# Small parameter rows ahead of the bulk loads on one queue, in a one-core inference step

## The reference

```
mod = silu(cond) @ ada_w + ada_b            # 6 vectors of 1024 each, for context and for latents
h   = rmsnorm(x) * norm1_g * (1 + sc1) + sh1
z   = h @ w_in                              # 1280 columns: 512 state space, 256 pooling, 512 convolution
y   = concat(ssm(z), pool(z), conv(z)) @ w_out
x   = x + g1 * y
h2  = rmsnorm(x) * norm2_g * (1 + sc2) + sh2
x   = x + g2 * ((silu(h2 @ w1) * (h2 @ w3)) @ w2)
out = rmsnorm(x) * final_g
```

## Time and profile before

| quantity | value |
|---|---|
| median of 3 runs | 1314.56 us (1313.19 to 1315.68) |
| the profiled execution, timed | 1311.89 us |
| its span, first to last instruction | 1310.0 us |
| PE busy | 1219.5 us (93%) |
| DVE, ACT, POOL busy | 857.4, 510.2, 521.7 us |
| mean granted TensorE clock | 0.975 of full speed |
| DMA | 268.52 MB, mean 205 GB/s |

### The profile page before, as it was taken

One profiled execution on the slowest core, in us unless ns is written; L12 is line 12 of the kernel. 1 busy time (PEld: TensorE's weight loads), 2 busy tenths in 40 slices (PEclk: granted clock), 3 DMA queues, 4 the chain that ended last, 5 costly groups with the idle time before them and its releaser, 6 DMA issues.

```text
span 1310.0 us, 21433 instructions
## 1 busy us (share of the span) xinstructions
PE 1219.5 (93%) x7574; PEld 1072.3 (82%) x7574; DVE 857.4 (65%) x1336; ACT 510.2 (39%) x911; POOL 521.7 (40%) x362
## 2 busy tenths in 40 slices
PE   3888899996699999899999999999999999999996
PEld 2478898786446888899999999999889999999995
DVE  2647959989944337667767666766855555555558
ACT  1464451126245547533333433433432333333223
POOL 0179425554343003455444445444533333333330
PEclk9889999997799999999999999999999999999998
DMA  8833345389872333766666576566677778777781
GB/s 273 313 110 120 114 140 177 102 109 229 270 290 97 104 121 102 252 226 229 219 208 211 189 256 224 213 219 220 237 232 250 240 260 277 255 249 264 242 279 73
DMA packets 189569, 268.52 MB, mean 205 GB/s; under 512 B 14030, under 2 KB 108536, under 8 KB 186824
## 3 DMA queue, kind: packets, MB, share of 16 engines
q1 hardware_dynamic: 187952, 263.00, 61.8%
q0 software_dynamic: 1280, 4.72, 0.9%
q10 hardware_dynamic: 280, 0.09, 0.0%
HBM read 186.49 MB, written 81.26 MB: 204 GB/s over the span
## 4 chain that ended last, share of the span: by engine, by line
PE 79%; DVE 8%; ACT 3%; DMA 3%; issue 3%; POOL 2%; SPq 1%; ACTq 0%; DVEq 0%; POOLq 0%
PE banks L891 22%; PE banks L893 22%; PE banks L892 22%; PE banks L1163 3%; PE banks L927 1%; PE banks L1042 1%; PE banks L976 1%; DMA dn<-in_ssm_d 1%; POOL sst L820 1%; PE banks L1059 1%; PE banks L1065 1%; PE banks L962 1%; ACT nts L1700 1%; DVE dsel L1959 1%; PE banks L935 1%
## 5 line engine op out<-in xcount | busy, mean ns | idle before, releaser
L843 POOL TENSOR_TENSOR raw13r<-raw13s,w13h 128x512 fp32r<-128x512 f32 x110 | 155.4, 1421 | 467.0 <-ACT w13h L1652 421.8
L892 PE MATMUL banks<-ntr,w13h 128*128 128x256 f32 (+1 forms) x1144 | 336.8, 294 | 0.0
L891 PE MATMUL banks<-ntr,w13h 128*128 128x256 f32 (+1 forms) x968 | 283.0, 292 | 3.4 <-POOL raw13r L843 2.2
L892 PEld LDWEIGHTS banks<-ntr,w13h 128*128 128x128 f32 x1144 | 215.9, 189 | 0.9
L891 PEld LDWEIGHTS banks<-ntr,w13h 128*128 128x128 f32 x968 | 183.0, 189 | 5.6 <-issue 2.5
L891 PE MATMUL banks<-f2h,f_hi 128*128 128x512 f32 x396 | 156.7, 396 | 0.4 <-DVE acc L2360 0.4
L893 PE MATMUL banks<-f2h,f_lo 128*128 128x512 f32 x396 | 156.2, 395 | 0.0
L892 PE MATMUL banks<-f2l,f_hi 128*128 128x512 f32 x396 | 156.2, 395 | 0.0
L893 PE MATMUL banks<-ntr,raw13r 128*128 128x256 f32 (+1 forms) x528 | 153.9, 291 | 0.0
L2226 DVE TENSOR_TENSOR acc<-acc,banks 128x512 f32<-128x512 f32 x170 | 112.9, 684 | 38.9 <-PE banks L893 30.8
L847 POOL TENSOR_TENSOR f2l<-f2s,f2h 128x1024 fp32r<-128x1024 f32 x44 | 106.3, 2437 | 34.7 <-ACT f2h L1656 34.7
(11 more groups left out here) (323 smaller groups left out, 2536.5 us busy)
## 6 DMA issues: line engine op xcount, KB each, us to landing
raw13s<-in_ffn_w SPq DMA_DIRECT2D x66, 512.0 KB, 4.5
parts<-w13h SPq DMA_DIRECT2D x110, 256.0 KB, 2.5
w13h<-parts SPq DMA_DIRECT2D x110, 256.0 KB, 2.8
f2s<-in_ffn_w SPq DMA_DIRECT2D x44, 512.0 KB, 4.2
ad<-in_ada_w SPq DMA_DIRECT2D x20, 1024.0 KB, 9.1
parts<-wsumr SPq DMA_DIRECT2D x66, 256.0 KB, 2.6
wsumr<-parts SPq DMA_DIRECT2D x55, 256.0 KB, 4.9
parts<-raw13r SPq DMA_DIRECT2D x44, 256.0 KB, 2.9
```

What stands on the lines that cost most here:

```text
L843: nc.gpsimd.tensor_tensor(w13_low(x, f), w13_low(x, f, F32), w13h[x][:, :, :].bitcast(F32), ALU.subtract).then_inc(sem("w13_lo"), 1)
L891: nc.tensor.matmul(out, hi_w, hi_x, start=start, stop=False)
L892: nc.tensor.matmul(out, hi_w, lo_x, start=False, stop=False)
```

## The change

Only the order and the issuing queue of loads in the front change. The loads of the two initial states, the taps and the skip vector move from ACT's queue to SP's, where they stand directly after the decay factors. The first two modulation tiles, which stood between the decay factors and the raw tables, move behind the position tables. There token and modulation tiles alternate: x0, tile 0, x1, tile 1, x2, tile 2, x3, tile 3. ACT keeps nine small loads. The same bytes are loaded into the same places, with the same semaphores.

```
         sp.dma_start(ldt[:, :], dview(A["ssm_log_dt"], 0, [[2, Q], [1, 2]])).then_inc(sem("log_dt_in"), 16)
-        for i, name in enumerate(("ssm_lam_re", "ssm_lam_im")):
+        for i, name in enumerate(("ssm_lam_re", "ssm_lam_im", "state_ssm_re", "state_ssm_im")):
             sp.dma_start(rlam[:, i, :], dview(A[name], 0, [[P, Q], [1, P]])).then_inc(sem("vectors_in"), 16)
-        ada_in(0)
-        ada_in(1)
+        sp.dma_start(rtap[:, :], dview(A["conv_dw_w"], 0, [[P, 2 * TAPS], [1, P]])).then_inc(sem("vectors_in"), 16)
+        sp.dma_start(dn[:, :], dview(A["ssm_d"], 0, [[32, NPAIR], [1, 32]])).then_inc(sem("vectors_in"), 16)
         for i, name in enumerate(("ssm_b_re", "ssm_b_im", "ssm_c_re", "ssm_c_im")):
             sp.dma_start(raw[i][:, :], dview(A[name], 0, [[2048, Q], [1, 2048]])).then_inc(sem("raws_in"), 16)
         sp.dma_start(pos_c[:, :], A["pos_cols"]).then_inc(sem("pos_in"), 16)
         sp.dma_start(pos_r[:, :], A["pos_rows"]).then_inc(sem("pos_in"), 16)
-        x_in(0)
-        ada_in(2)
-        x_in(1)
-        ada_in(3)
-        x_in(2)
-        x_in(3)
+        for n in range(4):
+            x_in(n)
+            ada_in(n)
         ada_in(4)
         ada_bias(0)
...
         for dst, src in SMALL:
             act.dma_start(dst(), src()).then_inc(sem("vectors_in"), 16)
-        for i, name in enumerate(("state_ssm_re", "state_ssm_im")):
-            act.dma_start(rlam[:, 2 + i, :], dview(A[name], 0, [[P, Q], [1, P]])).then_inc(sem("vectors_in"), 16)
-        act.dma_start(rtap[:, :], dview(A["conv_dw_w"], 0, [[P, 2 * TAPS], [1, P]])).then_inc(sem("vectors_in"), 16)
-        act.dma_start(dn[:, :], dview(A["ssm_d"], 0, [[32, NPAIR], [1, 32]])).then_inc(sem("vectors_in"), 16)
```

## The result

The changed kernel takes 1301.64 us (median of 4 executions, 1300.56 to 1302.41) against 1313.88 of the kernel before (4, 1312.15 to 1315.68). The ratio is 0.9906, with a 95% interval of 0.9889 to 0.9923: 12.2 us less, 0.94%. The profiled execution took 1300.56 us; the forecast for it was 1299.6 and for the median 1302.3. In a second measurement, with five executions of the changed kernel, it was 1300.83 against 1315.61 (0.9881, 0.9864 to 0.9899). The two medians give 12.2 and 14.8 us; by the intervals the gain is 10.1 to 14.6 us in the first measurement and 13.3 to 17.9 in the second.

The account below looks back on a forecast made before the run. A serial 20 us head, waiting for late parameter rows, was taken as the bound. The third position row at 32.3 instead of 44.58 gives 12.3 us: 1299.6 for the profiled execution, median 1302.3, range 1298.5 to 1307.5 (about 0.8).

Parts of the forecast that it names:

- The head is serial and the late parameter packets hold it: At the kernel's start, PE waits until 20.81 us for parameter rows whose packets trickle out between bulk packets.
- PE starts at 6.0: First PE instruction at 6.0 us in place of 20.81, with bounds of 5.5 and 9.
- Positions at 11.3: Both position tables land at 11.3 us, so `pos_columns` starts then instead of at 22.54; upper bound 12.5.
- the allowance of 0.4 for landing: Landing time in the position tables' sum, taken off `ldt`'s 1.8 us and added again at the end.
- the lower bound of 8.6: Earliest landing of the position tables, in us, if the raw tables can flow at 386 GB/s.
- DVE's 1.1 us vanish; the third position row at 32.3: PE no longer waits 1.1 us for DVE's first addition; third position row at 32.3 instead of 44.58, gaining 12.3 us.
- Moving tiles 0 and 1 back is covered: 10.7 us of raw transposes hide the later modulation tiles; without that cover it would cost 4.1 us.
- The second batch is late by nothing: Loads issued about 24.0 arrive in time: tiles 5 to 7, token tile 4, first weight tile; covers 1.3 to 2.2 us.
- a sign of being wrong: Listed signs: first PE instruction after 12 us, PE held by a modulation tile, or the cast held by its weight tile.
- The clock is taken at zero: Moved clock dips count nothing, though 3.4 us more could be gained or 2.3 us lost in 43.4 to 53.6.
- After it everything moves as a block: Behind the second batch of loads everything hangs on the chain and moves with it, the clock excepted.
- no change: Rival: load order does not matter, since queue, engines and bulk stay; moving issues saves only 1.9 us; chance 0.05.

Follow-up runs that it names:

- the second profile: The changed kernel once more, unchanged, timed beside the kernel before on one chip and profiled anew: 1300.83 us, ratio 0.9881.
- the last experiment: The changed kernel with the three DVE instructions that make `dsel` moved from behind the first normalised tiles to 8.4 us: 1303.38 us, ratio 0.989.

## Why the prediction was right, point by point

- *The head is serial and the late parameter packets hold it.* Right, and shown by itself: reordering ACT's own queue brings `pos_columns` 6.3 us forward (11.7 us in time, with the clock's part in it), cutting `rtap` 5.4 (4.9 in time).
- *PE starts at 6.0.* 6.55, and 6.18 in the second profile. ACT's nine rows set it, not the six of SP: from the last issue at 3.65 to PE's start it took 2.9 us, not the 1.8 of `ldt`.
- *Positions at 11.3.* 12.24 and 12.52, at the upper bound: the slow raw tables cost what the earlier trace rows said, their landings 1.3 us apart for 256 KB each, 200 GB/s. The two positions took 0.9 us behind them rather than 0.4. No row gave the allowance of 0.4 for landing, and the lower bound of 8.6 should read 8.9 by its own terms.
- *DVE's 1.1 us vanish; the third position row at 32.3.* 32.53, without a wait for DVE; 33.93 in the second profile, where tiles 0 to 2 ran longer at the lower level (5.35 us against 4.23). The gain at this point was 12.1 and 10.7 against 12.3.
- *Moving tiles 0 and 1 back is covered.* Right: tiles 0 to 2 start at 28.37 without a wait.
- *The second batch is late by nothing.* This step failed in part. It was issued at 25.07 rather than 24.0 and tile 7 landed at 39.65 rather than 38.4. It was also wanted at 38.32 rather than 40.6, because in full clock PE did tiles 3 to 6 sooner than I had reckoned. The cover of 2.2 us became a wait of 1.37, and of 0.19 in the second profile: PE was held by a modulation tile, which the prediction had named as a sign of being wrong. The weight tile landed at about 28.12 + 16.0 = 44.1 (forecast 44.3; 16.0 is the median of two tiles), and the first cast, at 45.94, followed ACT's work on the bias, so that cover held.
- *The clock is taken at zero.* The term was mis-sized. Between the third position row and the first product the distance was 33.5 and 30.3 us before, 29.4 and 26.5 after: some 4 us more were gained there in each pair. In that stretch PE runs the same instructions in all of these profiles. They kept it busy for 28.1 and 25.0 us before (granted clock 0.75 and 0.83) and for 23.8 and 20.8 after (0.88 and 1.00); the rest of the distance is 5.3 to 5.7 us in all four. So the difference is how long the same matmuls took, which is the clock. But a third profile of the same front, that of the last experiment, has 31.2 us with 25.2 busy (0.82), more than one of the two before: the term is a few microseconds, and differs from execution to execution by as much.
- *After it everything moves as a block.* Right within 5 us: from the first product to the end of the span 4.8 and 2.8 us were given back, 1.4 and 0.5 of it up to the first issue of `f2s`. The drift behind that lies where executions differ: the short wait for `parts` in the first pair; in the second the changed kernel spent 6.8 us at the lower level near 930 us and the kernel before 3.4.

The forecast of 12.3 is thus a head of 10.7 to 12.1, a term of a few microseconds behind it, the clock's, that I had left at zero, and a drift the other way that I had not reckoned either. That 12.3 came within 0.1 of the first measurement is in part luck; the second, 14.8, lies a little above it.

Of the rivals, "no change" went by a rule of the Trainium skill, page DMA: Bandwidth & Descriptors, section Issuing engines are not separate DMA queues: issuing from another engine saves issue time and no more. The runs agree with the sentence as it stands: `rtap` from ACT at 3.95 or from SP at 3.07 gives the same time (ratios 0.9882 and 0.9881). What it didn't reach is what was bought here: the place in time and in order, ahead of the bulk, which within ACT's queue alone was worth 6.3 us at `pos_columns` and 11.7 in time.

## What to carry to other kernels

Issue every small load that the first instruction waits for before the first bulk load of any queue; the issuing engine matters little, what already stands in the DMA engines matters much. Where two limits stand side by side (rows and tables), look which of them the next instruction meets after each is moved: here moving the two bulk tiles back brought 9.7 of the 10.3 us at `pos_columns`, moving the rows ahead 4.8. Leave room in the sum for the clock: here the time at its lower level differed by a few microseconds between executions of the same code. Then ask what the earlier engine meets next: here the stream of loads at 383 to 413 GB/s was the next bound, and starting PE earlier still brought waits and a lower clock, and no time.

## What the runs showed of the hardware

- The raw tables, 32 partitions of 8 KB, flow at 200 GB/s with the DMA engines shown fully busy, also when other loads are mixed in (0.20 MB of them for 19.8% of 5 us).
- A DVE instruction of 32x16 elements with both inputs in SBUF stood 8.00 us, from 116.13 to 124.13, while GpSimd ran its products back to back from 116.53 to 124.11; it took 0.16 us at 8.41, where GpSimd was idle. `gsc`, 128x16, took 1.37 beside a GpSimd instruction before and 0.17 behind it after (1.36 beside it again in the second profile after). The Trainium skill, page SBUF — State Buffer, section SBUF: two separate sides, says that the two engines share a port pair as an exclusive lock, and the loser is blocked entirely. The durations agree; that the lock is also handed from one GpSimd instruction to the next past a waiting DVE is what the 8 us suggest, and was not tried. The DVE instruction is listed 0.4 us ahead of the first of those products, while GpSimd was issuing transfers; why it did not run then is not shown.
- Two executions of the same code differ in where the lower clock falls: behind a wait of 1.37 us the granted clock was 0.56 in 42.4 to 49.2, behind one of 0.19 us it was 1.00. Profiles of one kernel differ by 1.6 to 3.2 us at the first product (61.96 and 60.41 after, 78.07 and 74.88 before), up to a quarter of the effect that was to be measured; with the last experiment's front, 64.46, by 4.1.
